# Gated first one-hots written in one step a token, three of four by GpSimd and the fourth by ScalarE; all second one-hots by VectorE

## The reference

```python
s1, s2 = ...                                    # scores of a token and head against two sets of 128 keys
t1, i1 = lax.top_k(s1, 16); t2, i2 = lax.top_k(s2, 16)
cand = t1[..., :, None] + t2[..., None, :]      # 256 candidates
top_s, top_c = lax.top_k(cand, 16)
e1 = take(i1, top_c // 16); e2 = take(i2, top_c % 16)
experts = e1 * 128 + e2                         # 16384 experts
gates = jax.nn.softmax(top_s, axis=-1)
act = gelu(einsum('td,ted->te', h, expert_u[experts]))   # 8 heads x 16 = 128 selected experts a token
out = einsum('te,ted->td', gates * act, expert_v[experts])
```

## Time and profile before

| | |
|---|---|
| median of 3 runs | 2082.67 us |
| lowest, highest | 2080.65, 2087.59 us |
| the profiled execution, its own time | 2079.7 us |
| span in its profile, first to last instruction | 2077.9 us |
| granted TensorE clock over the span | 0.996 of full speed |
| TensorE matmul busy | 2009.6 us (97%) |
| VectorE busy | 1636.4 us (79%) |
| ScalarE busy | 1013.7 us (49%) |
| GpSimd busy | 695.8 us (33%) |

### The profile page before, as it was taken

The page is one execution under the profiler, slowest core; times in us unless marked ns, Lnnn a source line. Parts: engine busy times, 40 slices in busy tenths (PEclk is TensorE's granted clock), DMA queues, the critical chain, the costliest instruction groups (busy, mean ns, idle before and its releaser), DMA issues.

```text
span 2077.9 us, 37215 instructions
## 1 busy us (share of the span) xinstructions
PE 2009.6 (97%) x11470; PEld 1667.8 (80%) x11470; DVE 1636.4 (79%) x3058; ACT 1013.7 (49%) x1728; POOL 695.8 (33%) x535
## 2 busy tenths in 40 slices
PE   7999999998999999999999999999899999999998
PEld 5764999987887888888867559999778788888887
DVE  6992899886779977777779739998867788777776
ACT  4443554695355444444444435547933544444443
POOL 6992667671000400000049917776700012000000
PEclk9999999999999999999999999999999999999999
DMA  5223554214567555555423145541055665555553
GB/s 197 94 72 144 196 165 158 100 39 152 192 217 278 183 188 189 189 189 188 148 93 102 57 176 190 178 158 63 32 197 191 206 217 182 192 192 183 192 191 132
DMA packets 91276, 332.52 MB, mean 160 GB/s; under 512 B 10499, under 2 KB 14723, under 8 KB 88620
## 3 DMA queue, kind: packets, MB, share of 16 engines
q1 hardware_dynamic: 91164, 331.32, 47.2%
q10 hardware_dynamic: 16, 0.02, 0.0%
HBM read 326.04 MB, written 3.16 MB: 158 GB/s over the span
## 4 chain that ended last, share of the span: by engine, by line
PE 55%; DVE 15%; POOL 10%; issue 10%; DVEq 8%; ACT 1%; DMA 0%; POOLq 0%; ACTq 0%; SPq 0%
PE ps L893 31%; PE ps L850 12%; PE ps L854 5%; DVE arena L1355 5%; POOL arena L1847 5%; POOL v_raw L1847 4%; PE ps L793 3%; POOL u_raw L1847 2%; DVEq L1688 2%; DVE arena L1655 2%; DVE arena L1648 2%; DVE arena L1649 1%; PE ps L627 1%; DVEq L1680 1%; DVEq L1770 1%
## 5 line engine op out<-in xcount | busy, mean ns | idle before, releaser
L893 PE MATMUL ps<-v_hl,w_hl 128*128 128x512 f32 x3072 | 729.3, 391 | 12.7 <-DVE v_hl L1355 8.5
L893 PEld LDWEIGHTS ps<-v_hl,w_hl 128*128 128x128 f32 x3072 | 573.8, 188 | 139.9 <-DVE v_hl L1355 15.4
L850 PE MATMUL ps<-h_hl,u_hl 128*128 128x512 f32 x1152 | 418.3, 397 | 0.0
L1847 POOL TENSOR_TENSOR arena<-arena 128x256 f32<-128x256 f32 (+1 forms) x225 | 214.0, 994 | 370.0 <-DVE arena L1355 367.2
L1355 DVE TENSOR_TENSOR v_hl<-v_raw,v_hl 128x1024 fp32r<-128x1024 f32 x208 | 258.6, 1243 | 49.5 <-ACT v_hl L1178 45.5
L854 PE MATMUL ps<-h_hl,u_hl 128*128 128x256 f32 x1008 | 282.6, 280 | 0.0
L1178 ACT ACTIVATE v_hl<-v_raw 128x1024 fp32r<-128x1024 f32 x208 | 219.0, 1053 | 111.8 <-PE ps L893 94.2
L1355 DVE TENSOR_TENSOR u_hl<-u_raw,u_hl 128x1024 fp32r<-128x1024 f32 x144 | 180.2, 1252 | 111.0 <-ACT u_hl L1147 111.0
L850 PEld LDWEIGHTS ps<-h_hl,u_hl 128*128 128x128 f32 x1152 | 216.4, 188 | 45.1
L1147 ACT ACTIVATE u_hl<-u_raw 128x1024 fp32r<-128x1024 f32 x144 | 152.3, 1058 | 132.6 <-PE ps L850 131.7
L1290 ACT ACTIVATE act_w<-act_w 128x256 f32<-128x256 f32 x144 | 60.3, 418 | 302.2 <-DVE act_w L1790 302.2
(11 more groups left out here) (182 smaller groups left out, 2978.0 us busy)
## 6 DMA issues: line engine op xcount, KB each, us to landing
v_raw<-in_expert_v SPq DMA_DIRECT2D x208, 512.0 KB, 3.3
u_raw<-in_expert_u SPq DMA_DIRECT2D x206, 512.0 KB, 3.4
v_raw<-in_expert_u SPq DMA_DIRECT2D x50, 512.0 KB, 3.4
u_raw<-in_expert_v SPq DMA_DIRECT2D x48, 512.0 KB, 3.3
arena<-in_w_in SPq DMA_DIRECT2D x16, 512.0 KB, 3.8
arena<-in_w_in SPq DMA_DIRECT2D x8, 1024.0 KB, 5.0
arena<-in_ssm_b SPq DMA_DIRECT2D x16, 512.0 KB, 4.2
arena<-in_w_out SPq DMA_DIRECT2D x4, 2048.0 KB, 9.5
```

The lines of the kernel that those rows point to most:

```text
L850: return pe.matmul(both, hl[:, 0, k, :], h_hl[:, :, k, :], start=(k == 0), stop=(k == DC - 1))
L893: m = pe.matmul(ps[:, 2 * a + half, :], w_hl[s][:, wp, a * P:(a + 1) * P], v_hl[s][:, vp, half * 512:(half + 1) * 512], start=(first and j ...
L1847: return pool.tensor_tensor(o, a, b, op)
```

## The change

GpSimd now writes the gated first one-hot of a token in one step, a `tensor_scalar` that compares the iota with e1 and multiplies by the gate, both taken as a column of 128 values. It does three tokens of each step. ScalarE does the fourth: one `Square` of (e1 - iota), a drain, and a `Relu` of gate - gate x distance, with the column `minus_g` as scale and the gate as bias. VectorE does the second one-hots of all steps, one instruction of 128x512 a step, and no first ones. `minus_g` costs one more copy of 128x256 on ScalarE ahead of the stage.

```diff
+        minus_g = side[:, 3 * S + HOT * PK:4 * S + HOT * PK]
...
                     pe.wait_ge(s_gates, batch + 2)
                     pe.wait_ge(s_gated, batch + 1)
-                    pe.wait_ge(s_hot2[t % 2], l * (N_BATCH // 2) + t // 2 + 1)
+                    pe.wait_ge(s_hot1, batch + 1)
+                    pe.wait_ge(s_hot2, batch + 1)
...
+                act.activation(minus_g, ps[:, 3, 0:S], ACT.Copy, scale=-1.0)
                 act.activation(sel_T[:, 2, :], ps[:, 3, 0:S], ACT.Copy).then_inc(s_selT, 1)
-                def hot_squares(t):
-                    if t > 1:
-                        act.wait_ge(s_hot2[1], l * (N_BATCH // 2) + t // 2)
-                    for j in range(HOT):
-                        o = t * HOT + j
-                        act.activation(apart[:, j, :], iota, ACT.Square, scale=-1.0, bias=sel_T[:, 1, o:o + 1])
-                def hot_second(t):
+                def hot_distance(t):
+                    o = t * HOT + HOT - 1
+                    act.activation(apart[:, t % 2, :], iota, ACT.Square, scale=-1.0, bias=sel_T[:, 0, o:o + 1])
+                def hot_gated(t):
+                    o = t * HOT + HOT - 1
                     act.drain()
                     act.wait_ge(s_hot_free, l * N_BATCH + t + 1)
-                    act.activation(hot2[t % BATCHES], apart[:, :, :], ACT.Relu, scale=-1.0, bias=one_c)\
-                        .then_inc(s_hot2[1], 1)
+                    act.activation(hot1[t % BATCHES][:, HOT - 1, :], apart[:, t % 2, :], ACT.Relu,
+                                   scale=minus_g[:, o:o + 1], bias=sel_T[:, 2, o:o + 1]).then_inc(s_hot1, 1)
...
-                hot_squares(1)
-                hot_second(1)
-                hot_squares(3)
+                act.wait_ge(s_u_lo, l * SPLIT + EARLY + FREE_AHEAD)
+                for t in range(3):
+                    hot_distance(t)
+                    hot_gated(t)
+                hot_distance(3)
                 for t in range(N_BATCH):
-                    if t % 2 == 0 and t + 3 < N_BATCH:
-                        hot_second(t + 3)
-                    if t % 2 and t + 4 < N_BATCH:
-                        hot_squares(t + 4)
+                    if t + 3 < N_BATCH:
+                        hot_gated(t + 3)
+                    if t + 4 < N_BATCH:
+                        hot_distance(t + 4)
...
-                def hot_firsts(t):
-                    dve.wait_ge(s_hot_free, l * N_BATCH + t + 2)
-                    tt(hot1_pair[t % BATCHES // 2], ps[:, 3, iota_ps_cols].unsqueeze(1).broadcast_to([P, 2 * HOT, PK]),
-                       sel_T[:, 0, t * HOT:(t + 2) * HOT].unsqueeze(2).broadcast_to([P, 2 * HOT, PK]),
-                       ALU.is_equal).then_inc(s_hot1, 2)
                 def hot_second(t):
-                    if t % 2 == 0:
-                        dve.wait_ge(s_hot_free, l * N_BATCH + t + 1)
-                        tt(hot2[t % BATCHES], ps[:, 3, iota_ps_cols].unsqueeze(1).broadcast_to([P, HOT, PK]),
-                           sel_T[:, 1, t * HOT:(t + 1) * HOT].unsqueeze(2).broadcast_to([P, HOT, PK]),
-                           ALU.is_equal).then_inc(s_hot2[0], 1)
+                    dve.wait_ge(s_hot_free, l * N_BATCH + t + 1)
+                    tt(hot2[t % BATCHES], ps[:, 3, iota_ps_cols].unsqueeze(1).broadcast_to([P, HOT, PK]),
+                       sel_T[:, 1, t * HOT:(t + 1) * HOT].unsqueeze(2).broadcast_to([P, HOT, PK]),
+                       ALU.is_equal).then_inc(s_hot2, 1)
...
+                pool.drain()
                 pool.wait_ge(s_selT, l + 1)
                 for t in range(N_BATCH):
-                    pool.wait_ge(s_hot1, l * N_BATCH + t + 1)
-                    tt(hot1[t % BATCHES], hot1[t % BATCHES], sel_T[:, 2, t * HOT:(t + 1) * HOT].unsqueeze(2)
-                       .broadcast_to([P, HOT, PK]), ALU.mult).then_inc(s_gated, 1)
+                    pool.wait_ge(s_hot_free, l * N_BATCH + t + 1)
+                    pool.sem_inc(s_gate_turn, 1)
+                    for j in range(HOT - 1):
+                        o = t * HOT + j
+                        m = pool.tensor_scalar(hot1[t % BATCHES][:, j, :], iota, sel_T[:, 0, o:o + 1],
+                                               sel_T[:, 2, o:o + 1], ALU.is_equal, ALU.mult)
+                    m.then_inc(s_gated, 1)
```

More of the change, by code:

```diff
@@ L116, in encoder @@
                 for b in range(BATCHES)]
-        hot1_pair = [v_raw[i].rearrange("p (j n) -> p j n", j=2 * HOT) for i in range(2)]
         hot2 = [rows.rearrange("p r t -> p (r t)").rearrange("p (j n) -> p j n", j=HOT)
@@ L325, in encoder @@
         s_hot1 = sem("s_hot1")
-        s_hot2 = [sem(f"s_hot2_{i}") for i in range(2)]
+        s_hot2 = sem("s_hot2")
+        s_gate_turn = sem("s_gate_turn")
         s_gated = sem("s_gated")
@@ L1732, in _ @@
                 dve.wait_ge(s_selT, l + 1)
-                dve.wait_ge(s_u_lo, l * SPLIT + EARLY + FREE_AHEAD)
-                hot_firsts(0)
                 hot_second(0)
@@ L1739, in _ @@
                     if t + 2 < N_BATCH:
-                        if t % 2 == 0:
-                            hot_firsts(t + 2)
                         hot_second(t + 2)
```

## The result

The changed kernel takes 2210.62 us (median of 4 runs, 2208.66 to 2211.83), against 2082.67 before. The ratio on record is 1.060, 95% interval 1.0579 to 1.0622: 6% slower (the two medians alone give 1.061). A fourth execution of the kernel before took 8475.55 us, four times the others, and is left out of its median. The profiled execution took 2208.66 us, its span is 2206.8 us, 128.9 more than the 2077.9 of before.

The account below looks back on a forecast made before the run. ScalarE was taken to bound the gate stage: 5.5 us from its shorter steps plus 1.1 tail, less 0.3 for waits, gives 6.3 us a layer, 12.6 in both, so 2070 us against 2082.67; range 2063 to 2098.

Parts of the forecast that it names:

- GpSimd, per step: Gate stage: three new 128x128 instructions at 0.34 us each, 1.0 us a step, covered by ScalarE's 1.26 up to 0.42 each.
- GpSimd becomes the bound: Slower rival in the gate stage: fetching two columns takes GpSimd's instruction past 0.44 us; at 0.50, 2108 us; chance 0.28.
- ScalarE's round: Gate stage: one copy, `Relu` and distance a step, 0.57 + 0.40 + 0.29 = 1.26 us in place of 1.345.
- TensorE reaches step 45: Gate stage: with 36 steps of 1.33 us and 9 of 0.89, TensorE gets there at 450.9 and is no obstacle.
- The head: Start of the gate stage: the extra `minus_g` copy, 0.38 us, costs nothing, covered by raw chunks; uncovered 0.4 us a layer.
- VectorE had slack: Gate stage: VectorE falls from 2.58 to 2.04 us a pair, 1.02 a step, under ScalarE's 1.26; nothing gained or lost.
- A gain is not given back: After the gate stage: the first down projection and all its loads shift with the stage, so the gain stays.
- ScalarE's program sets the pace: Gate stage before the change: ScalarE's gapless round of 2.69 us a pair, 1.345 a step, bounds it; GpSimd's waits have slack.

Follow-up runs that it names:

- one_column: Changed kernel with GpSimd's three instructions a step only comparing with the index column, the gate multiplication left out: 2132.46 us.
- one_token: Changed kernel with GpSimd writing only token 0 of each step, the one-hots of tokens 1 and 2 left out: 2074.4 us, ratio 0.9948 to the kernel before.
- moved_8: Kernel before the change, with second one-hots of one in four of ScalarE's steps made by VectorE, nothing left out: 2087.09 us, ratio 1.0007.
- no_columns: Changed kernel with GpSimd's three instructions a step comparing and multiplying by constants, token's index and gate left out: 2143.52 us.
- half_width: Changed kernel with GpSimd's three instructions a step over 64 elements in place of 128: 2126.34 us.
- one_wide: Changed kernel with one GpSimd instruction a step over 384 elements, using one token's columns, in place of three over 128: 2115.76 us.
- split_psum: Changed kernel with first one-hots split 1 on GpSimd, 2 on VectorE, 1 on ScalarE, VectorE reading the iota from PSUM: 2101.93 us, 1.0082 to before.
- split_211: Changed kernel with first one-hots split 1 on GpSimd, 2 on VectorE, 1 on ScalarE, VectorE reading the iota from SBUF: 2090.66 us, 1.0023 to before.
- split_sbuf: Changed kernel, GpSimd two tokens on even steps but the first, otherwise one; ScalarE one, VectorE the rest, iota from SBUF: 2072.97 us, 0.9947 to before.
- split_half: Changed kernel, GpSimd two tokens on even steps but the first, otherwise one; ScalarE one, VectorE the rest, iota from PSUM: 2083.88 us, 0.9994 to before.

## Why the prediction was wrong

**The step that failed** is "GpSimd, per step". I took 0.34 us for its instruction and 0.47 as the upper bound; it is 0.774. The bound came from 2.1 ns a column, read off two-input instructions, on the assumption that one input can only be cheaper. It is 3.4 ns with both operations, and by the sums above 2.5 ns even with the comparison alone (one_column), so the assumption fails before the second operation is counted. Why an element is that dear no run shows. The columns of values, put at nothing in the 0.34, cost 0.167. The fixed part, 0.20 in my row of one column, is 0.18. The row that was rightly there, 0.741 us for twice the columns, I set aside for an interpolation of it. Even it would have been below the truth.

**The rival was the right mechanism, its size was not.** "GpSimd becomes the bound" got 0.28 and was priced at 0.50 us an instruction, 2108 us. Its own arithmetic with 0.774 gives 64 x (2.32 - 1.335) = 63 us a layer, against 61.7 and 62.2 measured. The range ended at 2098, because it was cut at my bound of 0.47.

**The two estimates from the Trainium skill.** Its "GPSIMD Engine Reference" (Engine selection) calls one-input work on GpSimd roughly line-rate, and the estimate from that was 0.31 us. For this form the measurement is two and a half times that, and the measurement decides. The rule that I weighed against it (the Trainium skill, "GPSIMD Engine Reference", Performance pitfalls for Q7 kernels), an estimated 0.17 us for two small reads, fits the 0.167 of the two columns; that they are such reads no run shows.

**What held.** With GpSimd out of the way (one_token) ScalarE's round is 1.25 us where the sum had 1.26, with the terms 0.40, 0.29 and 0.56 for 0.40, 0.29 and 0.57. TensorE reaches step 45 at about 451 us, forecast 450.9. The stage became 6.2 us shorter in each layer, forecast 6.3. The head cost nothing: the first matmul of step 0 stands 399.13 - 393.82 = 5.31 us behind the transposes, 395.03 - 389.71 = 5.32 before. VectorE had slack (30.26 of 40 us busy in one_token).

**What failed beside it.** "A gain is not given back" was wrong: of one_token's 12.4 us about 5 were, by the two profiled executions, some 3.6 of them to TensorE's clock. And "ScalarE's program sets the pace" was half the truth. I took GpSimd's 21.1 us of waiting for slack because ScalarE had no gap, though the chain ran through GpSimd; moved_8 says a second bound lay at the same pace. An engine without gaps can be one bound of two. The forecast would have survived that, as one_token's 6.2 us a layer show.

## What to carry to other kernels

Before moving work to an engine, time the exact form there: operation count, operands and length. A rate read from another form is no upper bound, and where a price is multiplied by 384 instructions, a row twice as long belongs in the range as it stands. When several engines work in one round, look for the one without idle time in the stage's own windows, not for the one the waits name. When relieving one engine gains nothing, a second one stands at the same pace, so balance all of them by measured prices, and measure the balance: of four splits here one gained.

## What the runs showed of the hardware

- GpSimd's `TENSOR_SCALAR` of fp32 with compare and multiply costs 0.176 us, 0.167 for its two columns of values and 3.4 ns an element (64 to 384 elements, 128 partitions; changed kernel, no_columns, half_width, one_wide).
- VectorE's same instruction over 128 elements lasts 0.39 to 0.41 us from PSUM (split_psum), and from SBUF 0.33 at the least, with GpSimd's beside it up to 0.45 (split_211) and 0.51 (split_sbuf). GpSimd's own goes from 792 to 839 ns beside it (split_half, split_sbuf).
- The windows of the changed kernel show the clock granted at 0.57 from 510 to 520 us, so mostly at its lower level of 1.2 GHz; in the rounds ahead of that, from 501 to 508 us, TensorE had worked 1.13 us of each 2.32. Four matmuls then take 2.05 us in place of 1.13, and the pace of the stage doesn't change, since GpSimd sets it.

```profile
514.90 2.05 PE L961 MATMUL ps<-v_raw,act_w 128*128 128x128 f32 x8 [0.27 <-issue]
519.54 1.13 PE L961 MATMUL ps<-v_raw,w_hl 128*128 128x128 f32 x8 [0.56 <-issue]
```

- The two layers' first `TENSOR_SCALAR` comes with a `MODIFY_POOL_CONFIG` that the kernel before has only at its start. It cost nothing that the trace shows: the first three of the first layer last 790 to 791 ns. One of the 384 lasts 1837 ns where the median is 792, but it is the 183rd of the first layer, at 537.2 us, and TensorE's next step starts 1 us late behind it; why was not traced.

```profile
L1912 POOL TENSOR_SCALAR v_raw<-cst,side x384: 784/792/1837, 396.4 to 1632.8; 128x128 f32<-128x128 f32 x192
L1912 POOLq MODIFY_POOL_CONFIG  x4: 11/11/11, 396.3 to 1484.3; - x4
```

```profile
L1912 POOL TENSOR_SCALAR v_raw<-cst,side x3: 790/791/791, 396.4 to 398.0; 128x128 f32<-128x128 f32 x3
```
